# Two settling stages of a decoder step: the last tile's scale and bias moved to GpSimd, and the picking products put earlier in TensorE's order

## The chip, the cores and the metric

The program runs on one core of one Trainium2 chip. The metric is the device time of one execution in microseconds (us), and the median over runs is what counts. TensorE (PE in the profile) multiplies, VectorE (DVE), ScalarE (ACT) and GpSimd (POOL) do elementwise work, and SyncE (SP) issues most transfers.

## The reference

One inference step of a two-layer decoder trunk for 544 tokens (512 of a prompt and 8 x 4 of a sample group), 1024 wide. Each layer is a mixer, a post-norm, a hierarchical mixture of experts and a post-norm. The part that the change touches is the post-norm behind the mixer and the routing:

```python
def _layer_norm(x, g, b):
    mu = jnp.mean(xf, axis=-1, keepdims=True)
    var = jnp.mean(jnp.square(xf - mu), axis=-1, keepdims=True)
    return (xf - mu) * lax.rsqrt(var + LN_EPS) * g + b

def _hier_moe(x, w_coarse, b_coarse, w_fine, b_fine, w_gate_up, w_down):
    lc = xt @ w_coarse + b_coarse                    # 4 groups
    grp = jnp.argmax(lc, axis=-1)
    lf = einsum('nd,gde->nge', xt, w_fine) + b_fine  # 8 experts in each
    top_v, top_i = lax.top_k(lf_sel, TOP_FINE)       # 2 experts a token
    ...
    # for each expert: silu(x @ gate) * (x @ up) * gate_value, then @ w_down
```

All arrays are float32. A layer has 32 experts with 2 MB of gate and up weights and 1 MB of down weights each.

## The kernel before

`settle_and_experts` runs once in each layer (l = 0 and l = 1). Its first half, `settle_parts`, is called the settling stage here; its second half, `expert_parts`, runs the experts.

**The settling stage** goes over five tiles of tokens in the order `ORDER`: first the 32 sample rows (i = 0, tile t = 4), then four tiles of 128 prompt rows (i = 1 to 4). For each tile, PE multiplies the mixer's output by the output projection (`project`), DVE adds it to the residual (`add`) and takes the mean and variance, PE turns the tile (`flip`), ACT copies the turned tile out, and PE forms 36 router logits (`score`). ACT normalises the tile in place in two halves (L1776, semaphore `normed`), and DVE multiplies each half by gamma and adds beta (`affine`, L1596 and L1597, semaphore `final`). DVE ranks the logits into a choice of two experts (`choose`, a chain of some fifteen small instructions from L1602 to L1619, most of which read two operands in SBUF), PE counts how many tokens of the tiles so far go to each expert (`count`, L1444 and L1447), and DVE turns the counts into places (`position`) and into a one-hot matrix for the first pair of experts (`heat`, written to `G`, semaphore `hot`).

**Picking.** The first pair of experts does not wait for a gather through memory. Its 128 rows are picked out of the tiles in SBUF by one-hot products: `pick(i)` multiplies `G` of tile i with the two 512-wide halves of tile i and accumulates over the five tiles in the PSUM banks `pp[1]` and `pp[2]`. Those banks are shared with the projections: for `old` (layer 1) `pp[2]` holds the projection (3, 1) and `pp[1]` the projection (4, 1); in layer 0 it is the other way about. After `pick(4)`, ACT copies the two banks to SBUF (L1780), PE turns them (`first.x_T`, L2072), and `first.gate_up` (L2080) starts the first pair.

**The order of the engines' work is written by hand**, one list for each engine. Around the change PE's list reads: project (4, 1), flip (4, 1), a wait for `added` 8, count (3), score (4, 1), pick 0, pick 1, count (4), totals, pick 2, pick 3, pick 4, the products that wait for `tiled` (L1514, L1516), the turn, the first gate and up. DVE's list reads: choose (4), position (3), heat (3), the first half of affine (4), position (4), heat (4), the second half of affine (4), start_of (4), the tile counts (L1708, L1709), the tables. GpSimd has nothing between a memset at the start of the stage (L1386) and the first gather.

**Transfers.** SP issues the expert weights. Seven experts have room. `E.fill` loads experts 0 to 4; gate and up of experts 5 and 6 are issued when the last projection is done (`summed` 10); then SP waits for `final` of the last tile, stores its rows (L1379) and issues down of expert 5, waits for all stored rows and for `picked`, and issues down of expert 6 (L1275). From there on, `reload_up` and `reload_down` issue the weights of the next experts as PE has used the ones in their place (L1270), beginning when the first half of the first gate and up is done.

Of the kernel before, what the change touches and what calls it, by code (L numbers as in the profile page):

```python
# [15 lines left out]
ALU = mybir.AluOpType  # L16
# [8 lines left out]
ORDER = TILES[4:] + TILES[:4]  # L25
# [126 lines left out]
def tok0(t):  # L152
    return 128 * t
# [23 lines left out]
def sum_in_quarters(nc, out, N, lhsT, rhs):  # L177


    w = N // 4  # L180
    for k in range(KD):
        for q in range(4):
            last = nc.tensor.matmul(out[32 * q:32 * q + 32, 0:w], lhsT(k), rhs(k)[:, q * w:(q + 1) * w],
                                    start=(k == 0), stop=(k == KD - 1), tile_position=(0, 32 * q))
    return last
# [1121 lines left out]
def settle_parts(nc, s, place, C, X, lng, lnb, ln_T, mixT, w_dram, l, w_router, b_router, lg, xT, rows, E, back, done, ahead, first, old=None):  # L1307


    gb = E.wd[5][:, 0:2 * D].rearrange("p (a n) -> p a n", a=2)  # L1310
# [10 lines left out]
    sel, sel4, pick = place("sel", [128, 8]), place("sel4", [128, 8, 4]), place("pick", [128, 8])  # L1321
# [11 lines left out]
    G = E.xg[1][:, 0:640].rearrange("p (t n) -> p t n", t=5)  # L1333
# [6 lines left out]
    pp = ahead  # L1340

    def half_bank(i, h):
        if i == 0:
            return pp[2][:, 128 * h:128 * h + 128] if old else pp[h][:, 0:128]
        return pp[(2 * i + h - 2 if old else 2 * i + h) % 3][:, :]
# [9 lines left out]
    w_in = [s.sem(f"w_in{h}") for h in range(2)]  # L1355
    x_in = [s.sem(f"x_in{i}") for i in range(5)]
    hot, tables, picked, rows_out = (s.sem(x) for x in ("hot", "tables", "picked", "rows_out"))
    xt, x0, sl, hr = first.turned, first.x0, first.sl, first.hr

    def sync(sp):  # L1360
# [23 lines left out]

    def gpsimd(pool):
        nc.gpsimd.memset(E.xg[1][:, :], 0.0).then_inc(blank, 1)  # L1386
        pool.wait_ge(told, 1)
        pool.wait_ge(stored, 16 * 5)
        pool.wait_ge(xt, 1)
        E.rows(pool, rows, 1, s.kept[f"e{l}_rows1"])  # L1390
        pool.wait_ge(tables, 1)

    def tensor(pe):
        def project(i, h, ks):
            t, P = ORDER[i]
            if 2 * i + h < done:
                return
            if ks[0] == 0:
                pe.wait_ge(w_in[h], 16)
                if 2 * i + h >= (4 if old else 5):  # L1400
                    pe.wait_ge(added, 2 * i + h - 2)
            if t == 4:
                last = sum_in_quarters(nc, half_bank(0, h), 512, lambda k: mixT[:, k, 512:544], lambda k: w[h][:, k, :])
            else:
                for k in ks:
                    last = nc.tensor.matmul(half_bank(i, h)[:P, :], mixT[:, k, tok0(t):tok0(t) + P],  # L1406
                                            w[h][:, k, :], start=(k == 0), stop=(k == KD - 1))
            if ks[-1] == KD - 1:
                last.then_inc(summed, 1)
# [6 lines left out]
        def flip(i, h):  # L1416
            t, P = ORDER[i]
            pe.wait_ge(added, 2 * i + h + 1)
            if i >= 1:
                pe.wait_ge(T_out, 2 * i + h - 1)  # L1420
            for c in range(4):
                last = nc.tensor.transpose(pt[h][:, c * P:(c + 1) * P], X[:P, t, (4 * h + c) * 128:(4 * h + c + 1) * 128],
                                           C("ident")[:P, :P])
            last.then_inc(T_in, 1)

        def score(i, h):
            t, P = ORDER[i]
            pe.wait_ge(T_out, 2 * i + h + 1)
            if i == 0:
                pe.wait_ge(prepared_c, 1)  # L1430
            if i >= 2:
                pe.wait_ge(logit_c, i - 1)
            for k in range(4 * h, 4 * h + 4):
                last = nc.tensor.matmul(pm[i % 2][:P, 0:36], xT[:, k, tok0(t):tok0(t) + P],  # L1434
                                        wrg[:, k, :], start=(k == 0), stop=(k == KD - 1))
            if h == 1:
                last.then_inc(logits, 1)

        def count(i):
            pe.wait_ge(assigned, i + 1)  # L1440
            if i >= 1:
                pe.wait_ge(positioned, i)
            mine = A12[:, i, :]
            last = nc.tensor.matmul(pr[:, 32 * i:32 * i + 32], C("before"), mine,  # L1444
                                    start=(i == 0), stop=(i == 4), skip_group_check=True)
            for j in range(i + 1, 5):
                last = nc.tensor.matmul(pr[:, 32 * j:32 * j + 32], C("ones"), mine, start=False, stop=False,  # L1447
                                        skip_group_check=True)
            last.then_inc(ranked, 1)

        def totals():
            pe.wait_ge(logit_c, 4)
            pe.wait_ge(assigned, 5)
            for i in range(5):
                last = nc.tensor.matmul(pm[1][0:32, 0:8], A12[:, i, :], C("ones")[:, 0:8], start=(i == 0), stop=(i == 4))
            last.then_inc(counted, 1)

        def pick(i):
            t, P = ORDER[i]
            pe.wait_ge(hot, i + 1)  # L1460
            for h in range(2):
                pe.wait_ge(final, 2 * i + h + 1)
                last = nc.tensor.matmul(pp[1 + h][:, :], G[:P, i, :], X[:P, t, 512 * h:512 * h + 512], start=(i == 0), stop=(i == 4))  # L1463
                if i == 4:
                    last.then_inc(picked, 1)

# [19 lines left out]
        for i in range(2, 5):  # L1486
# [9 lines left out]
            if i < 4:  # L1496
# [2 lines left out]
        project(4, 1, second[:2])  # L1499
        score(4, 0)  # L1500
        project(4, 1, second[2:])
        flip(4, 1)
        pe.wait_ge(added, 8)
        count(3)
        score(4, 1)
        pick(0)
        pick(1)
        count(4)
        totals()
        pick(2)  # L1510
        pick(3)
        pick(4)
        pe.wait_ge(tiled, 1)
        nc.tensor.matmul(pm[0][:, 0:32], tilesT[:, 0:1].to_broadcast([32, 128]), C("before")[0:32, 0:32],  # L1514
                         start=True, stop=True)
        nc.tensor.matmul(pm[0][:, 32:64], tilesT[:, 0:1].to_broadcast([32, 128]), C("tri_p")[0:32, 0:32],  # L1516
                         start=True, stop=True).then_inc(placed, 1)
# [3 lines left out]
        for n in range(10):  # L1521
            if n in (0, 8):
                pe.wait_ge(onehots, n // 8 + 1)
            last = nc.tensor.matmul(pm[1][:, 0:NPAIR], onehot[n], ci[2][:, n, :], start=(n == 0), stop=(n == 9))
# [3 lines left out]
        for n in range(10):  # L1528
            last = nc.tensor.matmul(pr[:, 0:NPAIR], onehot[n], ci[1][:, n, :], start=(n == 0), stop=(n == 9))
# [3 lines left out]
    def vector(dve):  # L1533
# [52 lines left out]
            c.step(V.scalar_tensor_tensor(out=shift[:P, :], in0=csum[:P, :], scalar=nmr[:P, t:t + 1], in1=cbias[:P, :],  # L1586
                                          op0=ALU.mult, op1=ALU.add))

        def affine(i, halves=(0, 1)):
            t, P = ORDER[i]  # L1590
            if i == 0:
                dve.wait_ge(gb_in, 32)
            for h in halves:
                x = X[:P, t, 512 * h:512 * h + 512]
                dve.wait_ge(normed, 2 * i + h + 1)
                c.step(V.tensor_tensor(x, x, gb[:P, 0, 512 * h:512 * h + 512], ALU.mult))  # L1596
                V.tensor_tensor(x, x, gb[:P, 1, 512 * h:512 * h + 512], ALU.add).then_inc(final, 1)  # L1597
# [39 lines left out]
        def position(i):  # L1637
            t, P = ORDER[i]
            dve.wait_ge(ranked, i + 1)
            if i >= 1:  # L1640
                dve.wait_ge(positioned, i)
            c.step(V.tensor_tensor(own2[:, :, :], As[:, :, t, :],
                                   pr[:, 32 * i:32 * i + 32].unsqueeze(1).to_broadcast([128, 2, 32]), ALU.mult))
            c.add(V.tensor_reduce(rsel[:, :, t], own2[:, :, :], AX.X, ALU.add))
            V.scalar_tensor_tensor(out=slots[:, i, :], in0=pr[:, 32 * i:32 * i + 2], scalar=1.0, in1=A12[:, i, 0:2],
                                   op0=ALU.add, op1=ALU.mult).then_inc(positioned, 1)

        def heat(i):
            dve.wait_ge(positioned, i + 1)
            if i == 0:  # L1650
                dve.wait_ge(blank, 1)
            V.tensor_tensor(G[:, i, :].rearrange("p (e n) -> p e n", e=2), slots[:, i, :].unsqueeze(2).to_broadcast([128, 2, 64]),
                            C("first").unsqueeze(1).to_broadcast([128, 2, 64]), ALU.is_equal).then_inc(hot, 1)
# [44 lines left out]
        choose(4)  # L1698
        position(3)
        heat(3)  # L1700
        affine(4, (0,))
        position(4)
        heat(4)
        affine(4, (1,))
        c.wait()
        start_of(4)
        dve.wait_ge(counted, 1)
# [57 lines left out]
    def scalar(act):  # L1765
# [22 lines left out]
        act.wait_ge(tables, 1)  # L1788

    return (sync, gpsimd, tensor, vector, scalar), pt, pm, pr  # L1790


# [301 lines left out]
def settle_and_experts(nc, l, C, X, lng, lnb, ln_T, mixT, w_dram, w_router, b_router, lg, xT, xd, yd, E, back, done, ahead, old, y, y_in,  # L2094
# [3 lines left out]
    with Scope(nc, f"n{l}0") as s, Scope(nc, f"e{l}") as se:  # L2098
# [3 lines left out]
        def place(name, shape):  # L2102
# [6 lines left out]
            if len(shape) == 4:  # L2109
                return v.rearrange("p (a b c) -> p a b c", a=shape[1], b=shape[2])  # L2110
            return v

        first = FirstPair(nc, se, C, E, xT, ahead[0:2], ahead[2])
        (sync1, pool1, pe1, dve1, act1), px, py, unread = settle_parts(nc, s, place, C, X, lng, lnb, ln_T, mixT, w_dram, l, w_router,
                                                               b_router, lg, xT, xd, E, back, done, ahead, first, old)
        sync2, pool2, pe2, dve2, act2 = expert_parts(nc, se, C, X, E, xT, xd, yd, first, px, py, unread,
# [1101 lines left out]
```

## Time and profile before

| what | value |
|---|---|
| three timed runs, us | 1198.03, 1202.74, 1202.96 |
| median of the runs, us | 1202.74 |
| the profiled execution, its own time, us | 1193.56 |
| its span, first to last instruction, us | 1191.7 |
| mean granted clock of TensorE | 0.969 |
| settling stage of layer 0, its tail | about 305 to 334 us |
| settling stage of layer 1, its tail | about 891 to 920 us |

The profile is of one execution. A busy share is a mean over stages that have different limits. In the timeline a row is a run of equal instructions merged: its start, the time from the first start to the last end, engine, line, operation, tiles, shape and, in brackets, the idle time before the first of them and what ended it. PE's products and its weight loads (PEld) are separate rows. A float32 product of 512 columns is two instructions in the trace. A clock of 1.00 is 2.4 GHz, one of 0.50 is 1.2 GHz.

### The profile page before, as it was taken

What the parts mean: (1) busy time and instruction counts of PE and PEld (TensorE: products, weight loads), DVE (VectorE), ACT (ScalarE), POOL (GpSimd) and SP (SyncE); (2) the same over time, 40 slices, a digit from 0 to 9 for tenths busy, and PEclk for the clock granted to TensorE, in tenths of its full rate; (3) what the DMA queues carried; (4) which work ended last, traced back from release to release, by engine and by line L of the source; (5) the groups of instructions that cost most, each with busy time, mean ns of one, the idle gap of its engine ahead of it and who ended that gap; (6) DMA issues with size and microseconds to landing.
All of it is one profiled execution on the core that took longest, in us unless ns stands there. A gap on an engine that the chain in (4) does not pass through costs nothing. (4 is left out here: it accounts for less than half of the span.)

```text
span 1191.7 us, 15251 instructions
## 1 busy us (share of the span) xinstructions
PE 1084.7 (91%) x5783; PEld 537.6 (45%) x5783; DVE 499.2 (42%) x1368; ACT 230.8 (19%) x515; POOL 181.2 (15%) x177
## 2 busy tenths in 40 slices
PE   8999999999999998778899999999999999877972
PEld 6874555555543333222544346554545433322320
DVE  3714576668652221112562314564677322111126
ACT  0311133321121110000421122333212111000103
POOL 0000000000011120110546532230000121111113
PEclk9999999999999998899899999999999999989995
DMA  8421020439489999997989979795886999999976
GB/s 296 164 92 44 37 111 1 151 118 422 192 323 413 420 420 421 419 421 297 356 335 360 369 293 401 288 379 195 319 367 235 358 411 418 420 421 420 422 291 227
DMA packets 85068, 358.84 MB, mean 301 GB/s; under 512 B 13928, under 2 KB 18157, under 8 KB 55293
## 3 DMA queue, kind: packets, MB, share of 16 engines
q1 hardware_dynamic: 63388, 279.57, 58.9%
q0 software_dynamic: 19520, 74.01, 16.0%
q10 hardware_dynamic: 2080, 4.19, 1.0%
q8 instruction: 51, 0.84, 0.3%
q14 instruction: 29, 0.23, 0.1%
HBM read 342.75 MB, written 31.16 MB: 314 GB/s over the span
## 5 line engine op out<-in xcount | busy, mean ns | idle before, releaser
L1915 PE MATMUL ahead_psum<-m_wg,top_xT 128*64 128x512 f32 x704 | 197.8, 624 | 30.0 <-DMA m_wg<-in_moe_w_gate_up 20.9
L1915 PEld LDWEIGHTS ahead_psum<-m_wg,top_xT 128*64 128x64 f32 x704 | 60.3, 143 | 140.2 <-issue 101.1
L1940 PE MATMUL n_psum_m<-m_wd,top_xT 128*64 128x512 f32 x456 | 120.4, 598 | 1.7 <-DMA m_wd<-in_moe_w_down 0.7
L1915 PE MATMUL ahead_psum<-top_wide,top_xT 128*64 128x512 f32 x288 | 100.3, 630 | 15.1 <-DMA top_wide<-in_moe_w_gate_up 8.1
L1406 PE MATMUL ahead_psum<-top_wide,top_xT 128*128 128x512 f32 x224 | 102.1, 599 | 1.5 <-PEq L159 1.5
L1980 DVE COPY top_xT<-n_psum_t 128x512 f32<-128x512 f32 x31 | 21.4, 691 | 172.2 <-PE n_psum_t L1900 172.2
L1835 POOL DMA_INDIRECT expert_rows<-e_Y,m_dest x33 | 32.8, 995 | 366.9 <-DVE e_Y L1989 329.4
L2382 PE MATMUL ahead_psum<-top_wide,top_xT 128*128 128x512 f32 x192 | 85.4, 596 | 0.3 <-ACT top_xT L2673 0.3
L2171 POOL DMA_INDIRECT cd_kv<-in_cache_kT,top_kpages x64 | 63.7, 995 | 49.3 <-PE cd_psum_d L2425 30.4
L1940 PEld LDWEIGHTS n_psum_m<-m_wd,top_xT 128*64 128x64 f32 x456 | 34.9, 136 | 55.6 <-issue 51.8
L2031 DVE TENSOR_TENSOR top_xT<-top_xT,ahead_psum 128x256 f32<-128x256 f32 x31 | 13.0, 420 | 111.4 <-ACT top_xT L2003 108.3
L1406 PEld LDWEIGHTS ahead_psum<-top_wide,top_xT 128*128 128x128 f32 x224 | 40.5, 190 | 42.6 <-issue 42.5
L557 PE MATMUL ab_psum<-top_wide,top_xT 128*128 128x512 f32 x128 | 57.9, 601 | 0.0
L1915 PEld LDWEIGHTS ahead_psum<-top_wide,top_xT 128*64 128x64 f32 x288 | 30.0, 145 | 59.1 <-issue 40.3
L2382 PEld LDWEIGHTS ahead_psum<-top_wide,top_xT 128*128 128x128 f32 x192 | 35.4, 190 | 45.0 <-issue 44.2
L2003 ACT ACTIVATE top_xT<-ahead_psum 128x256 f32<-128x256 f32 x31 | 11.9, 384 | 189.4 <-PE ahead_psum L1915 186.2
L1386 POOL MEMSET m_xg<- 128x1024 f32 x2 | 1.9, 952 | 288.7 <-POOLq L159 288.7
L1998 ACT ACTIVATE top_xT<-ahead_psum 128x256 f32<-128x256 f32 x33 | 12.7, 384 | 169.9 <-PE ahead_psum L1926 169.9
L1302 POOL DMA_INDIRECT m_xg<-token_rows,m_tokof x15 | 15.5, 1033 | 180.5 <-DVE m_tokof L1741 176.5
L2180 POOL DMA_INDIRECT cd_kv<-in_cache_v,top_pages x32 | 30.7, 958 | 76.5 <-PE cd_psum_e L2466 52.2
L1989 DVE SCALAR_TENSOR_TENSOR e_Y<-n_psum_m,m_share,m_xg 128x512 f32<-128x512 f32 x34 | 25.5, 751 | 38.4 <-PE n_psum_m L1940 38.4
L1989 DVE SCALAR_TENSOR_TENSOR e_Y<-n_psum_m,m_share,top_X 128x512 f32<-128x512 f32 x32 | 24.0, 751 | 35.9 <-PE n_psum_m L1940 35.9
(535 smaller groups left out, 1664.9 us busy)
## 6 DMA issues: line engine op xcount, KB each, us to landing
m_wg<-in_moe_w_gate_up SPq DMA_DIRECT2D x96, 1024.0 KB, 25.3
m_wd<-in_moe_w_down SPq DMA_DIRECT2D x56, 1024.0 KB, 26.9
top_wide<-in_moe_w_gate_up SPq DMA_DIRECT2D x32, 1024.0 KB, 28.7
cd_kv<-in_cache_kT SPq DMA_DIRECT2D x64, 256.0 KB
top_X<-in_moe_w_down SPq DMA_DIRECT2D x8, 1024.0 KB, 29.0
ab_w<-in_ab_w_in SPq DMA_DIRECT2D x2, 2048.0 KB
top_wide<-in_ab_w_in SPq DMA_DIRECT2D x2, 2048.0 KB, 7.9
top_wide<-in_ab_w_out SPq DMA_DIRECT2D x2, 2048.0 KB, 9.0
```

The lines of the kernel that those rows point to most:

```text
L557: last = mm(out[:, :], xT[:, k, tok0(t):tok0(t) + 128], w[i][:, k, :], start=(k == 0), stop=(k == KD - 1))
L1302: pool.indirect_dma_start(out=self.xg[i % 4][:, :], out_offset=None, in_=xd, in_offset=bass.IndirectOffsetOnAxis(ap=self.tokof[:, i:i + 1] ...
L1406: last = nc.tensor.matmul(half_bank(i, h)[:P, :], mixT[:, k, tok0(t):tok0(t) + P], w[h][:, k, :], start=(k == 0), stop=(k == KD - 1))
L1835: nc.gpsimd.indirect_dma_start(out=yd, in_=Y[i % 2][:, :], in_offset=None, out_offset=bass.IndirectOffsetOnAxis(ap=E.dest[:, i:i + 1], axi ...
L1915: last = nc.tensor.matmul(pg[i % 2][64 * a:64 * a + 64, :], xgT[i % 2][:, j, 64 * a:64 * a + 64], wg[E.slot(i, a)][:, j * 512:(j + 1) * 51 ...
L1940: last = nc.tensor.matmul(py[n2][64 * a:64 * a + 64, :], hT[:, j, 64 * a:64 * a + 64], wd[E.slot(i, a)][:, j * D + n2 * 512:j * D + (n2 + ...
L1980: ins = nc.scalar.activation(dst, src, ACT.Copy) if half == 0 else nc.vector.tensor_copy(dst, src)
L1989: last = nc.vector.scalar_tensor_tensor(out=Y[i % 2][:, part], in0=py[half][:, :], scalar=E.share[:, i:i + 1], in1=xg[i % 4][:, part], op0 ...
L2031: nc.vector.tensor_tensor(hh, sg, pg[i % 2][:, DE:2 * DE], ALU.mult).then_inc(hr, 1)
L2171: pool.indirect_dma_start(out=self.slots[slot][:, b, 512 * j:512 * j + 512], out_offset=None, in_=self.k_rows, in_offset=bass.IndirectOffs ...
L2180: pool.indirect_dma_start(out=self.slots[slot][:, b, :], out_offset=None, in_=self.v_rows, in_offset=bass.IndirectOffsetOnAxis(ap=self.pag ...
L2382: last = nc.tensor.matmul(out[:, :], xT[:, k, tok0(t):tok0(t) + 128], w[r][:, k, :], start=(k == 0), stop=(k == KD - 1))
```

## The change

It has four parts, and all of them are made in both settling stages.

1. `affine(4)` leaves DVE. GpSimd does it: for each half it waits for `normed`, multiplies by gamma, waits for its own instruction through a new semaphore, and adds beta. These are four instructions of 128 x 512 elements.
2. One half of `pick(0)`, into the bank that is already free (the product over the half that goes to `pp[2]` in layer 1 and `pp[1]` in layer 0), stands ahead of `flip(4, 1)`, and so does the wait for `added` 8.
3. `pick(2)` stands ahead of `count(4)`. Behind `totals` only `pick(3)` and `pick(4)` are left.
4. `pick` reads all 128 partitions of `G` and of the tile, for the 32-row tile too.

```diff
+    last_scaled = s.sem("last_scaled")
...
     def gpsimd(pool):
         nc.gpsimd.memset(E.xg[1][:, :], 0.0).then_inc(blank, 1)
+        pool.wait_ge(gb_in, 32)
+        for h in range(2):
+            x, (g, b) = X[:, ORDER[4][0], 512 * h:512 * h + 512], (gb[:, a, 512 * h:512 * h + 512] for a in range(2))
+            pool.wait_ge(normed, 9 + h)
+            nc.gpsimd.tensor_tensor(x, x, g, ALU.mult).then_inc(last_scaled, 1)
+            pool.wait_ge(last_scaled, h + 1)
+            nc.gpsimd.tensor_tensor(x, x, b, ALU.add).then_inc(final, 1)
         pool.wait_ge(told, 1)
...
-        def pick(i):
+        def pick(i, halves=(0, 1)):
             t, P = ORDER[i]
             pe.wait_ge(hot, i + 1)
-            for h in range(2):
+            for h in halves:
                 pe.wait_ge(final, 2 * i + h + 1)
-                last = nc.tensor.matmul(pp[1 + h][:, :], G[:P, i, :], X[:P, t, 512 * h:512 * h + 512], start=(i == 0), stop=(i == 4))
+                last = nc.tensor.matmul(pp[1 + h][:, :], G[:, i, :], X[:, t, 512 * h:512 * h + 512], start=(i == 0), stop=(i == 4))
...
         project(4, 1, second[2:])
+        pe.wait_ge(added, 8)
+        pick(0, (1,) if old else (0,))
         flip(4, 1)
-        pe.wait_ge(added, 8)
         count(3)
         score(4, 1)
-        pick(0)
+        pick(0, (0,) if old else (1,))
         pick(1)
+        pick(2)
         count(4)
         totals()
-        pick(2)
         pick(3)
         pick(4)
...
         heat(3)
-        affine(4, (0,))
         position(4)
         heat(4)
-        affine(4, (1,))
         c.wait()
         start_of(4)
```

## Rows read from the trace of the kernel before

**Rows 1.** The page, part 1: busy time, share of the span, instructions.

```profile
PE 1084.7 (91%) x5783; PEld 537.6 (45%) x5783; DVE 499.2 (42%) x1368; ACT 230.8 (19%) x515; POOL 181.2 (15%) x177
```

**Rows 2.** The chain that ended last, in order of time, layer 1's tail: start, duration, what.

```profile
907.90 0.27 DVE top_lg L1602
...
912.33 0.38 PE n_psum_r L1444 x2
912.71 0.41 PE n_psum_m L1455 x10
913.12 5.36 PE ahead_psum L1463 x12
918.50 0.61 ACT m_xg L1780
```

**Rows 3.** The timeline of layer 1's tail, all engines.

```profile
905.36 0.66 PE L1422 MATMUL n_psum_t<-top_consts,top_X 128*128 128x128 f32 x4 [0.78 <-DVE top_X L1551]
...
907.22 1.52 ACT L1776 ACTIVATE top_X<-top_X,e_Y 128x512 f32<-128x512 f32 x2 [0.48 <-DVE e_Y L1575]
...
907.72 3.89 PE L1463 MATMUL ahead_psum<-top_X,m_xg 32*128 32x512 f32 x8
...
908.19 0.17 DVE L1226 TENSOR_TENSOR e_Y<-top_lg 128x16 f32<-128x16 f32 x1
...
909.31 0.20 DVE L1608 TENSOR_TENSOR e_Y<-top_lg,e_Y 128x32 f32<-128x32 f32 x1
...
912.33 0.38 PE L1444 MATMUL n_psum_r<-e_Y,top_consts 128*128 128x32 f32 x2 [0.71 <-DVE e_Y L1645]
912.42 0.68 DVE L1596 TENSOR_TENSOR top_X<-top_X,m_wd 128x512 f32<-128x512 f32 x1
...
915.25 0.69 DVE L1597 TENSOR_TENSOR top_X<-top_X,m_wd 128x512 f32<-128x512 f32 x1
...
915.97 0.33 SPq L1379 DMA_DIRECT2D token_rows<-top_X  x1
...
924.78 6.74 SPq L1270 DMA_DIRECT2D m_wg<-in_moe_w_gate_up  x4
```

**Rows 4.** The timeline of layer 0's tail, PE alone.

```profile
321.85 5.54 PE L1463 MATMUL ahead_psum<-top_X,m_xg 32*128 32x512 f32 x8
...
327.23 0.31 PE L1444 MATMUL n_psum_r<-e_Y,top_consts 128*128 128x32 f32 x2
```

**Rows 5.** Windows of 1 us: busy time by engine, PE's clock, DMA share, GB/s.

```profile
322.00:323.00 1.00, 1.00 (x3) 0.51 (x4) 0.86 (x5) 0.88 (x2) 0.00 (x0) 1.00 1.01 426
...
324.00:325.00 1.00, 1.00 (x3) 0.48 (x3) 0.90 (x5) 0.00 (x0) 0.00 (x0) 0.50 0.99 418
```

**Rows 6.** GpSimd's groups of instructions by line and shape.

```profile
L204 POOL TENSOR_TENSOR m_wg<-m_wg 128x1024 f32<-128x1024 f32 x4 | 9.4, 2344 | 9.3 <-DMA m_wg<-expert_rows 9.2
L2331 POOL TENSOR_TENSOR cd_kv<-cd_kv 128x1024 f32<-128x1024 f32 x3 | 7.1, 2355 | 13.4 <-DMA cd_kv<-expert_rows 13.3
```

**Rows 7.** The timeline of the last stage, VectorE and GpSimd.

```profile
1179.24 2.35 POOL L204 TENSOR_TENSOR m_wg<-m_wg 128x1024 f32<-128x1024 f32 x1 [0.16 <-DMA m_wg<-expert_rows]
...
1180.09 1.28 DVE L279 SCALAR_TENSOR_TENSOR top_X<-m_wg,n_mv,n_psum_g 128x1024 f32<-128x1024 f32 x1
...
1183.05 1.28 DVE L279 SCALAR_TENSOR_TENSOR top_X<-m_wg,n_mv,n_psum_g 128x1024 f32<-128x1024 f32 x1
```

**Rows 8.** The timeline of PE among the experts: sixteen equal products after idle time.

```profile
434.19 3.65 PE L1915 MATMUL ahead_psum<-m_wg,top_xT 128*64 128x512 f32 x16 [1.86 <-DMA m_wg<-in_moe_w_gate_up]
...
483.70 5.35 PE L1915 MATMUL ahead_psum<-m_wg,top_xT 128*64 128x512 f32 x16 [4.47 <-DMA m_wg<-in_moe_w_gate_up]
...
1065.77 6.24 PE L1915 MATMUL ahead_psum<-m_wg,top_xT 128*64 128x512 f32 x16 [4.78 <-DMA m_wg<-in_moe_w_gate_up]
```

**Rows 9.** Windows of 10 us among the experts, columns as in rows 5.

```profile
370.00:380.00 10.00, 10.00 (x52) 3.97 (x50) 1.86 (x3) 1.37 (x3) 2.02 (x2) 1.00 1.01 417
...
960.00:970.00 10.00, 10.00 (x52) 3.99 (x50) 2.19 (x3) 0.98 (x2) 1.58 (x2) 1.00 1.01 416
```

More of the change, by code:

```diff
@@ L1587, in shift_of, with affine @@
                                           op0=ALU.mult, op1=ALU.add))
-        def affine(i, halves=(0, 1)):
+        def affine(i):
             t, P = ORDER[i]
@@ L1592, in affine @@
                 dve.wait_ge(gb_in, 32)
-            for h in halves:
+            for h in range(2):
                 x = X[:P, t, 512 * h:512 * h + 512]
```

## The prediction

> **What bounds the kernel now.** I read the page's first part, then the chain that ended last, then the timeline at the place of the change. PE is busy 91% of the span and GpSimd 15% [rows 1], but a mean says nothing about one stage. The chain in order of time does: in the settling stage's tail it passes through VectorE's choice (it enters it at 907.90), through PE's last count, the totals and the twelve instructions of pick 2 to 4, and into ACT's copy at 918.50 [rows 2]. Behind that come the turn and the first gate and up, whose first half releases the first reload of weights at 924.78 [rows 3]. Some 35 us later the DMA engines are full, at 416 to 417 GB/s, and stay so nearly to the end of the experts, in both layers [rows 9]; PE then waits for weights. So the tail counts because it sets when the reloads begin: a microsecond there moves the whole stream of weights by about one, and this happens twice, once in each layer. What PE loses or gains once the stream is full costs nothing.
>
> **Half of pick 0 ahead of the last turn.** Its matrix and its half were ready long before, and its bank is free. PE stands idle for 0.78 us ahead of the turn, waiting for VectorE's add [rows 3]. A picking product is two instructions, and twelve instructions take 5.36 us [rows 2], of which some 0.2 is the last one's tail, so one is 0.43 and the half is 0.86. It covers the gap and reaches 0.08 past it. The turn, the logits and the choice start 0.08 later. Cost: +0.08 a stage.
>
> **Pick 2 ahead of the last count.** Pick 0 and 1 run from 907.72 for 3.89 us, to 911.61; then PE is idle for 0.71 until VectorE's position (L1645) releases the count at 912.33 [rows 3]. After the change five products, ten instructions, stand there: 4.3 us from 907.80, to 912.1. That fits ahead of 912.33. Behind the totals eight instructions are left in place of twelve: −4 x 0.43 = −1.73 us a stage. This is the gain, and it holds only while the count is released no later than before.
>
> **All rows read.** Eight instructions took 3.89 rather than 8 x 0.43 = 3.44 [rows 3]; the 0.45 is a pause where 32 partitions turn into 128. It goes, but into a stretch where PE waits for VectorE anyway: nothing, apart from making pick 2 fit.
>
> **Affine 4 leaves VectorE.** There it was four instructions of 0.68 and 0.69 [rows 3], 2.8 us, half of them under PE's last count, the rest under its picks. VectorE's later work (position 4, heat 4, the tile counts) comes earlier by 0.8 to 2.1 us; PE reaches the products that read it only after pick 4, so this gives nothing by itself, but it keeps up with the shorter picks. SP's store of the last tile, now at 915.97 [rows 3], follows GpSimd.
>
> **Affine 4 on GpSimd.** A tensor_tensor of 1024 columns takes 2.34 to 2.36 us there [rows 6]; of 512 I take half, 1.17. ACT's two normalised halves begin at 907.22 and take 1.52 together [rows 3], so the first is out at 907.98. Four instructions with 0.1 to 0.15 between them are done at about 913.2. Pick 4 would want its last half at about 915.8, so GpSimd itself is in time by 2.5 us. The first gather queued behind it waits for later things.
>
> **What it does to VectorE** is the disputed price. The four instructions run from 908.07 to 913.2, on top of the choice, which is on the path and whose instructions mostly read two operands in SBUF (L1226 at 908.19 to L1608 and on) [rows 3]. The trace has GpSimd arithmetic only beside VectorE instructions with at most one such operand: L279, whose second operand is in PSUM, takes 1.28 beside a running L204 and 1.28 without one [rows 7]. So this trace shows no price for two operands. The lower bound is nothing, by rows 7. The upper one is that neither engine runs while the other does, so that VectorE waits out each GpSimd instruction. L1226, due at 908.27, then waits to 909.25; it and L1227 slip through between multiply and add; L1228 waits for the add, L1229 for the second multiply, and L1608 for the second add, to 913.4 in place of 909.31. That is +4.1 us for the choice; with no slipping through it is 5. I take the upper bound, 4.1: two streams of operands for each engine are nearest to a case of full exclusion, and the row that shows no price has only one stream. The rule that I weigh against rows 7 is in the Trainium skill, "SBUF — State Buffer", Who interferes with whom: a VectorE instruction with two SBUF inputs and a GpSimd instruction that reads SBUF exclude each other for the whole instruction. By it the sum is the upper bound's; by the plain reading of rows 7 it is the lower's. No row here tests it.
>
> Then the count starts at 912.33 + 4.1 = 916.4, and the net of the stage is +4.1 − 1.73 = **+2.4 us** (the 0.08 is lost in rounding).
>
> **The clock.** PE would be idle from 912.1 to 916.4, 4.3 us. Among the experts the sixteen products that take 3.65 us after an idle time of 1.86 take 5.35 after 4.47 and 6.24 after 4.78 [rows 8]: the granted clock fell to 1.2 GHz. So idle time of this length costs 1.7 to 2.6 more, here on the path; I take 1.7. In layer 0 a fall is there already: the clock was 1.00 at 322 and 0.50 at 324 [rows 5], the four products took 5.54 [rows 4] in place of 3.89, and the count began 5.38 behind the first pick in place of 4.61 [rows 3, 4], 0.77 late, which I take off.
>
> **Sum.** 2 x (2.4 + 1.7) − 0.7 = **+7.5 us** against the profiled execution: 1193.6 + 7.5 = 1201.1. That execution is 9 us below the median of the three runs, 1202.7. The same 7.5 on the median gives **1210** us, 0.6% slower.
>
> **Rivals.**
>
> A, the forecast: the engines exclude each other and the clock falls. +5.5 to +11 (the upper end with a wait of 5 and a fall of 2.6: 2 x (5 − 1.7 + 2.6) − 0.7). For it: the choice overlaps all four GpSimd instructions, and has more than enough two-operand steps to meet each. Against it: no row shows the exclusion. Chance 0.42.
>
> B, they hinder each other in part, or the clock stays up: a wait of 1.7 to 4.1 without a fall, 0 to +5 us. The point that decides the sign is a delay of the choice by 1.65 us a stage, one and a half GpSimd instructions. Chance 0.14.
>
> C, the other side: they run freely beside each other. Then each stage gains 1.73 − 0.08 = 1.65, 3.3 in all, and up to 4.0 if pick 0 in PE's gap also keeps layer 0's clock up: 1198.7 to 1199.4 on the median. For it: rows 7. Its gain is under 0.5%. Chance 0.38.
>
> D, the gain does not reach the end or GpSimd is late (over 1.8 us for one instruction makes pick 4 wait): −1 to +1. Against it: rows 6 and the full stream [rows 9]. Chance 0.06.
>
> **How the numbers follow.** The three runs lie within 5 us, 0.4%; about 0.5%, 6 us, is what a measurement of this kernel can tell from no change. Slower by more than that is nearly all of A: 0.42. Faster by more than that needs C and something that I have not priced, or a lucky set of runs: 0.12. The rest is 0.46. The range reaches from C with 1.5 us for the runs' spread, 1197, to A with the wider wait and fall, 1214. By itself A gives 1208 to 1214, C 1197 to 1201.
>
> **What the profile after would show.** For the forecast: L1226, L1228 or their like starting only as a GpSimd row on the new lines ends; the choice (L1602 to L1619) taking about 8 us in place of 3.8; PE idle for some 4 us ahead of the last count; a clock of 0.50 in the picks behind it. For C: the choice as long as before, the count within 0.1 us of its old place, ACT's L1780 1.65 earlier. The GpSimd rows should be 1.1 to 1.3 us each; at 2 us or more both sums are wrong. The flip of the last half should start less than 0.2 us after VectorE's add ends. The time from ACT's last copy to the first reload should be what it was, 6.3 us [rows 2, 3]; otherwise the tail is not where the difference was made. The prediction is wrong above all if the exclusion is not there, or if a wait ends in the middle of a GpSimd instruction.

## The result and the profile after

The changed kernel takes 1209.84 us, median of 6 runs (1208.4 to 1210.7); the kernel before, 1202.85, median of 6. The ratio is 1.0052, 95% interval 1.0027 to 1.0077: **slower by 6 to 7 us**, 0.5 to 0.6% (3.2 to 9.3 us by the interval). The prediction was 1210, and 7.5 us for the difference. The ratios leave out executions in a slower state of the chip, of which affine_back_2 had one, at 2127 us.

The timeline of the changed kernel in layer 1's tail, which answers to [rows 3]. Line numbers have moved: L1596 and L1597 of `affine` are L1605 and L1606, GpSimd's new lines are L1392 (multiply) and L1394 (add), pick is L1471, the last count L1452.

```profile
912.81 0.66 PE L1430 MATMUL n_psum_t<-top_consts,top_X 128*128 128x128 f32 x4
...
914.67 1.52 ACT L1783 ACTIVATE top_X<-top_X,e_Y 128x512 f32<-128x512 f32 x2 [0.48 <-DVE e_Y L1584]
...
915.06 4.54 PE L1471 MATMUL ahead_psum<-top_X,m_xg 128*128 128x512 f32 x10
...
915.63 0.17 DVE L1226 TENSOR_TENSOR e_Y<-top_lg 128x16 f32<-128x16 f32 x1
915.63 1.30 POOL L1392 TENSOR_TENSOR top_X<-top_X,m_wd 128x512 f32<-128x512 f32 x1 [70.18 <-ACT top_X L1783]
915.72 1.24 DVE L1227 TENSOR_TENSOR e_Y<-top_lg 128x16 f32<-128x16 f32 x1
917.00 0.17 DVE L1228 TENSOR_TENSOR e_Y<-e_Y,top_consts 128x16 f32<-128x16 f32 x1
917.01 1.29 POOL L1394 TENSOR_TENSOR top_X<-top_X,m_wd 128x512 f32<-128x512 f32 x1
917.21 1.13 DVE L1229 TENSOR_TENSOR e_Y<-e_Y 128x16 f32<-128x16 f32 x1
918.26 1.26 POOL L1392 TENSOR_TENSOR top_X<-top_X,m_wd 128x512 f32<-128x512 f32 x1
918.37 0.17 DVE L1230 TENSOR_REDUCE e_Y<-e_Y 128x4 f32<-128x16 f32 x1
918.57 0.98 DVE L1616 TENSOR_SCALAR e_Y<-e_Y 128x4 f32<-128x4 f32 x1
919.59 0.20 DVE L1617 TENSOR_TENSOR e_Y<-top_lg,e_Y 128x32 f32<-128x32 f32 x1
919.60 1.30 POOL L1394 TENSOR_TENSOR top_X<-top_X,m_wd 128x512 f32<-128x512 f32 x1
...
920.05 0.93 DVE L1226 TENSOR_TENSOR e_Y<-e_Y 128x64 f32<-128x64 f32 x1
...
923.33 0.38 PE L1452 MATMUL n_psum_r<-e_Y,top_consts 128*128 128x32 f32 x2 [3.72 <-DVE e_Y L1654]
...
924.18 5.19 PE L1471 MATMUL ahead_psum<-top_X,m_xg 128*128 128x512 f32 x8
...
935.67 6.74 SPq L1270 DMA_DIRECT2D m_wg<-in_moe_w_gate_up  x4
```

The reader is to see that L1227, L1229 and L1616, of 16 or 4 elements a partition, which took 0.17 us, now take 1.24, 1.13 and 0.98, that the second L1226, of 64 elements, takes 0.93 in place of 0.22, and that each of the four ends with a GpSimd instruction, within 0.1 us. A blocked instruction counts as busy, so a list of idle times would not have shown it: VectorE has no idle row here. Idle time appears one engine further on, 3.72 us of PE ahead of the last count. Behind it eight instructions take 5.19 us, where ten took 4.54 a moment before.

Layer 0's tail is the same, with the full length of the forecast: L1226, L1228, L1229 and L1616 take 1.29, 1.22, 1.19 and 1.09 us there.

```profile
330.38 0.60 PE L1452 MATMUL n_psum_r<-e_Y,top_consts 128*128 128x32 f32 x2 [4.29 <-DVE e_Y L1654]
...
331.55 6.24 PE L1471 MATMUL ahead_psum<-top_X,m_xg 128*128 128x512 f32 x8
```

Windows of 1 us there (columns as in rows 5), in PE's idle time and after it: the granted clock goes from 1.00 to 0.50.

```profile
328.00:329.00 1.00, 0.00 (x0) 0.00 (x0) 0.86 (x6) 0.00 (x0) 0.00 (x0) 1.00 0.95 401
...
332.00:333.00 1.00, 1.00 (x2) 0.39 (x2) 0.86 (x7) 0.00 (x0) 0.00 (x0) 0.50 1.02 430
```

GpSimd's groups after, which answer to [rows 6]:

```profile
L1394 POOL TENSOR_TENSOR top_X<-top_X,m_wd 128x512 f32<-128x512 f32 x4 | 5.1, 1277 | 0.3
L1392 POOL TENSOR_TENSOR top_X<-top_X,m_wd 128x512 f32<-128x512 f32 x4 | 5.1, 1273 | 135.1 <-ACT top_X L1783 135.1
```

**A measure for one tail.** From the issue of the last gate and up load of the fill, which SP makes as the last projection ends, to the first reload (the first and the last SP row of the tail): 20.86 and 20.16 us before (layer 0, layer 1), 25.55 and 23.62 after. So the two tails give 4.7 + 3.5 = 8.2 us. From the start of ACT's last copy to the first reload it is 6.27 or 6.28 us in both kernels and both layers, so the difference lies ahead of that copy. The profiled spans differ by more, 1206.2 − 1191.7 = 14.5; the rest lies elsewhere. The execution profiled before was 9 us under its own median, the one after less than 2.

### The profile page after: what moved, and what is told of

Read it like the earlier page. It is cut to its first block and busy times, and to the rows that moved or that the text cites. A ratio compares the mean times of both kernels' runs of the same rounds, so it can differ in the third digit from the quotient of the medians.

```text
span 1206.2 us, 15255 instructions
## 1 busy us (share of the span) xinstructions
PE 1094.3 (91%) x5783; PEld 542.1 (45%) x5783; DVE 502.0 (42%) x1360; ACT 230.7 (19%) x515; POOL 191.2 (16%) x185
## 5 line engine op out<-in xcount | busy, mean ns | idle before, releaser
L1947 PE MATMUL n_psum_m<-m_wd,top_xT 128*64 128x512 f32 x456 | 123.8, 614 | 1.6 <-ACT top_xT L2005 1.0
L2010 ACT ACTIVATE top_xT<-ahead_psum 128x256 f32<-128x256 f32 x31 | 11.9, 383 | 187.2 <-PE ahead_psum L1922 187.2
L557 PEld LDWEIGHTS ab_psum<-top_wide,top_xT 128*128 128x128 f32 x128 | 23.4, 190 | 28.8 <-issue 27.0
```

The source lines that it names most:

```text
L557: last = mm(out[:, :], xT[:, k, tok0(t):tok0(t) + 128], w[i][:, k, :], start=(k == 0), stop=(k == KD - 1))
L1947: last = nc.tensor.matmul(py[n2][64 * a:64 * a + 64, :], hT[:, j, 64 * a:64 * a + 64], wd[E.slot(i, a)][:, j * D + n2 * 512:j * D + (n2 + ...
```

## The experiments

The table has, for each kernel, the length of the choice of the last tile, PE's idle time ahead of the last count, the tail as measured above (layer 0 / layer 1 each time), and the ratio to the kernel before with its interval. Each length is from one profiled execution. Three kernels ran once and have no ratio.

| kernel | choice, us | PE idle, us | tail, us | ratio |
|---|---|---|---|---|
| before | 3.83 / 3.83 | 0 / 0.71 | 20.86 / 20.16 | 1 |
| after | 7.94 / 7.38 | 4.29 / 3.72 | 25.55 / 23.62 | 1.0052 (1.0027 to 1.0077) |
| affine_back | 3.84 / 3.84 | 0.19 / 0.18 | 18.84 / 18.83 | 0.9965 (0.9941 to 0.9988) |
| affine_back_2 | 3.84 / 3.83 | 0.19 / 0.18 | 18.84 / 18.83 | 0.9948 (0.9919 to 0.9977) |
| gpsimd_alone | 7.94 / 7.38 | 2.19 / 2.62 | 27.07 / 25.33 | 1.0086 (1.0055 to 1.0117) |
| kept_clock | 7.94 / 7.39 | 0.86 / 0.29 | 22.58 / 22.00 | 1.0016 (0.9993 to 1.0039) |
| one_half | 6.01 / 5.88 | 2.36 / 2.21 | 22.30 / 20.49 | 1.0013 (0.9991 to 1.0035) |
| write_only | 4.06 / 4.07 | 0.41 / 0.41 | 19.06 / 19.07 | one execution |
| read_one | 5.90 / 5.90 | 2.25 / 2.24 | 22.22 / 21.21 | one execution |
| after_choice | 3.84 / 3.84 | 0.19 / 0.18 | 19.98 / 22.87 | 0.9970 (0.9951 to 0.9989) |
| rows_alone | 3.85 / 3.83 | 1.06 / 0 | 20.19 / 20.57 | one execution |
| half_ahead_alone | 3.84 / 3.84 | 0.44 / 0 | 22.19 / 23.44 | 0.9984 (0.9960 to 1.0008) |
| pick2_alone | 3.84 / 3.84 | 0 / 0 | 22.55 / 22.55 | 0.9992 (0.9965 to 1.0019) |
| slots_first | 3.84 / 3.84 | 0 / 0 | 18.61 / 20.30 | 0.9965 (0.9946 to 0.9984) |

**affine_back**: the change without its first part.

```diff
 # the changed kernel; GpSimd's four instructions and their waits go as well
         heat(3)
+        affine(4, (0,))
         position(4)
         heat(4)
+        affine(4, (1,))
```

> The changed kernel with the last tile's scale and bias back on VectorE, where it was before; the other three parts stay (half of pick 0 ahead of the turn, pick 2 ahead of the last count, all rows read). Exclusion theory: no GpSimd row in the tail, so the choice takes about 3.7 us again in both layers, PE waits under 0.4 us for the last count, the clock stays at 1.00, and ACT's first copy of the picked rows starts 1.7 us earlier than before relative to the turn; 3.3 to 4 us faster than before in time, so about 10 us faster than the change. Rival, that the cost comes from the new order of the picks on PE (the half pick ahead of the turn, or three picks in a row ahead of the count): then this stays slower than before, by up to 7 us. Second rival, that a shorter tail doesn't reach the end: same as before within 1 us.

The choice is back at 3.84 us and the tails are 2.0 and 1.3 us below before's. PE alone, layer 1:

```profile
901.50 4.54 PE L1463 MATMUL ahead_psum<-top_X,m_xg 128*128 128x512 f32 x10
906.22 0.38 PE L1444 MATMUL n_psum_r<-e_Y,top_consts 128*128 128x32 f32 x2 [0.18 <-DVE e_Y L1646]
...
906.94 4.07 PE L1463 MATMUL ahead_psum<-top_X,m_xg 128*128 128x512 f32 x8
```

This kernel is faster than both. Both rivals fall: the three parts on PE help, and the time is shorter by 4.2 us (1.3 to 7.0). Repeated on another chip it was faster again:

> The kernel of affine_back again, to be compared on one chip with the next three. Expected from the first time: the tails (last projection's end to the first reload of weights) 18.8 us each, 2.0 and 1.3 below before; the time 3 to 5 us below before.

**gpsimd_alone**: the kernel before with GpSimd's `affine(4)` and nothing else.

```diff
 # the kernel before
+        pool.wait_ge(gb_in, 32)
+        for h in range(2):
...
+            nc.gpsimd.tensor_tensor(x, x, g, ALU.mult).then_inc(last_scaled, 1)
...
+            nc.gpsimd.tensor_tensor(x, x, b, ALU.add).then_inc(final, 1)
-        affine(4)
```

> The kernel before with one part of the change alone: the last tile's scale and bias on GpSimd. Exclusion theory: the choice is 3.5 to 4.1 us longer, PE is idle for 4.3 to 4.8 us ahead of the last count (pick 2 isn't there to fill 0.8 of it), the clock falls, and all six picking products stand behind the count at 1.2 GHz: about 1.7 us a stage worse than the change, so 10 to 11 us slower than before. Rival (the order of the picks costs the time): same as before, or up to 1 us faster because VectorE has less to do.

The choice lengths are those of the changed kernel to 0.01 us, and the kernel is 0.86% slower, 10 us, as expected. The first part alone makes the whole loss. PE's idle time was 2.2 to 2.6 us rather than the 4.3 to 4.8 expected, because the clock had already fallen during pick 0 and 1, which took 6.54 and 5.54 us.

**one_half** (in the changed kernel, GpSimd does the first half only, two instructions in place of four):

```diff
-        for h in range(2):
+        for h in (0,):
...
         heat(4)
+        dve.wait_ge(final, 9)
+        affine(4, (1,))
```

> The changed kernel with the first half of the last tile's scale and bias on GpSimd (two instructions in place of four), and the second half on VectorE behind its last position. Exclusion theory: the delay of the choice goes with the number of GpSimd instructions, so it is about 2.0 us in place of 4.1 and 3.6, PE is idle for about 2 us, which is too short for the clock to fall; each stage comes out 0.3 us worse than before: the same as before within 1.5 us. Rival (a fixed cost of starting GpSimd arithmetic in the tail, such as code loading): the delay stays near 4 us and the time 6 to 7 us above before.

The choice is 2.2 and 2.05 us longer than before's: half of 4.1 and of 3.6, within 0.3. The delay goes with the number of GpSimd's instructions; a fixed cost could be 0.2 to 0.6 us of it, not 4. In one point the expectation failed: after 2.36 us idle the clock did fall in layer 0, and the eight instructions took 5.37; after 2.21 in layer 1 it did not, and they took 3.70.

**write_only** and **read_one** put other GpSimd work of similar length into the same stretch of affine_back.

```diff
 # write_only
+        for h in range(2):
+            pool.wait_ge(normed, 9 + h)
+            for n in range(6):
+                nc.gpsimd.memset(E.xg[1][:, 640:1024], 0.0).then_inc(filled[h], 1)
+                pool.wait_ge(filled[h], n + 1)
 # read_one, in place of the memset
+                nc.gpsimd.tensor_copy(E.xg[1][:, 640:1024].rearrange("p (a n) -> p a n", a=3),
+                                      C("ident").unsqueeze(1).to_broadcast([128, 3, 128])).then_inc(filled[h], 1)
```

> The kernel of affine_back with twelve GpSimd memsets of 128 x 384 (results unused) in the stretch where the change has its four tensor_tensor: GpSimd is as busy, but reads nothing from SBUF. Theory that VectorE's second operand needs the read path that GpSimd reads through: the two-operand instructions of the choice keep their 0.17 to 0.22 us, and only instructions of one SBUF operand that may use both paths (L1616, L1621) can be longer; the choice stays at 3.7 to 4.3 us. Rival, that any GpSimd instruction shuts VectorE's two-operand instructions out: they end only with a memset, and the choice takes over 5 us.

> As write_only, but with twelve GpSimd tensor_copy of 128 x 384, which read one operand from SBUF. Theory of the shared read path, held for a whole instruction: VectorE's two-operand instructions of the choice wait for the copy in progress (each of the copies costs up to its own length, some 0.4 us), and the choice takes 6 to 8 us. Rival, that only two-operand instructions on both sides exclude each other: the choice stays at 3.7 us.

The timelines of layer 0's choice, write_only first (its memsets run from 322.10 to 327.75), then read_one:

```profile
322.21 0.17 DVE L1226 TENSOR_TENSOR e_Y<-top_lg 128x16 f32<-128x16 f32 x1
...
323.12 0.37 DVE L1614 TENSOR_SCALAR e_Y<-e_Y 128x4 f32<-128x4 f32 x1
```

```profile
321.94 0.43 DVE L1226 TENSOR_TENSOR e_Y<-top_lg 128x16 f32<-128x16 f32 x1
...
323.39 0.17 DVE L1614 TENSOR_SCALAR e_Y<-e_Y 128x4 f32<-128x4 f32 x1
323.59 0.54 DVE L1615 TENSOR_TENSOR e_Y<-top_lg,e_Y 128x32 f32<-128x32 f32 x1
```

GpSimd works all through the choice in both, with twelve memsets of 0.42 us or twelve copies of 0.51. Beside memsets, which read nothing, every two-operand instruction keeps its length and the choice costs 0.2 us more, all of it in a one-operand instruction. Beside copies the two-operand ones that meet a copy stretch to as much as 0.54, the others keep 0.16 or 0.17 (L1227 and L1229 in layer 0), and the choice takes 5.9, a little less than the 6 to 8 expected. So it is GpSimd's reading that shuts VectorE's second operand out. The Trainium skill, "SBUF — State Buffer", Who interferes with whom, states this, with the exemption for writing; by that rule these two traces agree.

**kept_clock** fills PE's idle time in the changed kernel.

```diff
         pick(2)
+        for _ in range(4):
+            nc.tensor.matmul(pt[0][:, :], C("ident"), X[:, ORDER[1][0], 0:512], start=True, stop=True)
         count(4)
```

> The changed kernel with four more products (unused results, 3.4 us at full clock) on PE between pick 2 and the last count, where it stands idle for 4.3 and 3.7 us. It does the same work otherwise. Theory that the idle time lets the clock fall and that this costs on its own: the clock stays at 1.00 behind the count, the eight instructions of pick 3 and 4 take 3.6 us in place of 6.2 and 5.2, and the time is 3 to 4 us less than the change's (3 to 4 us slower than before). Rival (the clock's fall is hidden by something else that waits, the weights' stream for one): the picks get shorter but the time stays at the change's, 7 us slower than before.

The picks behind the count, layer 0, against 6.24 in the changed kernel:

```profile
330.70 3.70 PE L1471 MATMUL ahead_psum<-top_X,m_xg 128*128 128x512 f32 x8
```

The tails lose 3.0 and 1.6 us, 4.6 in all, and the ratio goes from 1.0052 to 1.0016, which is 4.3 us. The clock is a cost of its own. That it reaches the end rests on the tails and the time together: the intervals of the two ratios overlap (1.0027 to 1.0077, 0.9993 to 1.0039).

**after_choice** holds GpSimd, in the changed kernel, until the choice is done.

```diff
         pool.wait_ge(gb_in, 32)
+        pool.wait_ge(assigned, 5)
         for h in range(2):
```

> The changed kernel with GpSimd's four instructions held until the choice of the last tile is done. Exclusion theory: the choice takes 3.7 us again and the count comes on time; GpSimd's 5.2 us then end 5.3 us behind the choice, where pick 4 wants its last half about 4 us behind it, so PE waits some 1.3 us there, and VectorE's two-operand instructions behind the choice (heat, start_of) are hit, position 4 and heat 4 some 1 to 2 us late: each stage comes out between 0.5 us better than before and 1 us worse, the time within 2 us of before. Rival, that GpSimd's arithmetic costs the same wherever it stands in the tail: 7 us slower, as the change.

The same four instructions in another place: the choice takes 3.84, the count comes on time, and the kernel is faster than before by 0.3%. PE waits for the last add, 0.96 us in layer 1:

```profile
920.43 1.13 PE L1472 MATMUL ahead_psum<-top_X,m_xg 128*128 128x512 f32 x2 [0.96 <-POOL top_X L1395]
```

So the place decides, not the work. Layer 0's tail is 1.1 us longer than affine_back's; the times (0.9970 and 0.9965) do not tell the two apart. In layer 1 the clock fell behind the picks, after gaps that were the same as layer 0's to 0.01 us: the sixteen instructions of the first gate and up took 6.05 us in place of 3.65, hence 22.87. The two tails together are then 1.8 us longer than the profiled ones of before, though the time is shorter; what this says of that profile stands under the clock below.

**The other parts one by one**, each put into the kernel before.

```diff
 # rows_alone
-                last = nc.tensor.matmul(pp[1 + h][:, :], G[:P, i, :], X[:P, t, 512 * h:512 * h + 512], ...
+                last = nc.tensor.matmul(pp[1 + h][:, :], G[:, i, :], X[:, t, 512 * h:512 * h + 512], ...
 # half_ahead_alone
+        pe.wait_ge(added, 8)
+        pick(0, (1,) if old else (0,))
         flip(4, 1)
-        pe.wait_ge(added, 8)
...
-        pick(0)
+        pick(0, (0,) if old else (1,))
 # pick2_alone
+        pick(2)
         count(4)
-        pick(2)
```

> The kernel before with one part of the change alone: the picks read all 128 partitions for the 32-row tile too. Expected: the pause of 0.45 us between pick 0 and pick 1 goes, the eight instructions take 3.5 us in place of 3.9, PE waits 1.1 us in place of 0.7 for the last count, and nothing behind it moves. Rival, that a product over 128 partitions takes longer than one over 32: eight instructions still take 3.9 us or more.

> The kernel before with one part alone: half of pick 0 ahead of the turn. Expected: PE's idle time ahead of the turn goes and the turn starts no later; the picks ahead of the count end 0.9 us earlier, to no use. Theory on the clock: that idle time is what lets the clock fall in this place in some executions (in 4 of 6 tails without the half ahead, in none of 14 with it), so here it stays at 1.00 in both layers, both tails take 20.1 to 20.2 us, and the time is 0 to 1.5 us below before. Rival: the falls are chance, and one of the two tails shows one.

> The kernel before with one part alone: pick 2 ahead of the last count, with pick 0 whole behind the logits and read in 32 rows. Theory: the six products take 5.6 us from 3.1 us behind the last projection's end, so the count starts at 8.7 in place of 7.7, and 1.7 us fewer are left behind it: the tail is 0.7 us shorter than before's, 19.4 where the clock holds, and the clock can fall as before (then 21 or more). Time within 2 us of before. Rival: the parts add up, each giving its share of the 1.7 us whatever the others do; then this one gives all of it, a tail of 18.5 us.

Reading all rows shortens the eight instructions of pick 0 and 1 in layer 0 to 3.68 us from 3.89, not to the 3.5 expected, and starts them 0.09 earlier; in layer 1 the clock fell in them. The half alone, in 32 rows, delays the turn by 0.2 us, and the expectation about the clock failed outright: it fell in both layers. Pick 2 alone stands in a stretch at half clock in both layers, and the count comes 11.9 us behind the last projection in place of 7.7. Layer 0 of the two, PE alone:

```profile
322.31 4.19 PE L1463 MATMUL ahead_psum<-top_X,m_xg 32*128 32x512 f32 x6
```

```profile
321.51 8.96 PE L1463 MATMUL ahead_psum<-top_X,m_xg 32*128 32x512 f32 x12
```

The rival that each part gives its share is wrong in the traces: by it pick2_alone's tails would be 18.5 us, and they are 22.55. Over all profiled tails, the clock fell during the picks ahead of the count in 8 of 10 where the half was not ahead of the turn or the picks read 32 rows, and in none of the 18 that had both. Neither part alone held it in both layers. The count was made afterwards, and why the two together hold the clock stays open. In time half_ahead_alone and pick2_alone are the same as before, though their tails are 4 to 5 us longer in sum; the falls may differ from one execution to the next, and one profile does not show how often.

**slots_first** changes VectorE's order in affine_back: the slots of tiles 3 and 4, `scalar_tensor_tensor` of `position`, come ahead of the rest of it.

```diff
-        position(3)
+        place_slots(3)
         heat(3)
         affine(4, (0,))
-        position(4)
+        place_slots(4)
         heat(4)
         affine(4, (1,))
+        position(3, False)
+        c.wait()
+        position(4, False)
```

> The kernel of affine_back with VectorE's list changed in the tail: of position 3 and position 4 only the instruction that the one-hot matrix and the count need stands where it was, the two others of each are moved behind the last tile's second half. Theory that VectorE's order sets both remaining waits of PE: the count starts 0.2 us earlier, right behind pick 2, and pick 4 no longer waits 0.4 us for its last half; the tail is 0.4 to 0.6 us shorter than affine_back's, 18.3, and the time about 1 us less, which the rounds can't tell from nothing. Rival: the moved instructions now delay the tile counts, PE waits for them behind the picks, and the tail stays at 18.8.

The count starts 0.36 us earlier and pick 4 no longer waits, but layer 0's tail is only 0.2 shorter, since PE now waits for the moved instructions (0.66 us ahead of L1515, released by L1721). So the theory holds for the two waits that were to go, and the rival for the one that comes in their place. In layer 1 the clock fell in the first gate and up (5.35 us in place of 3.65), which costs more than that. On the same chip affine_back_2 has 0.9948 and this 0.9965, within each other's interval. The change shows no gain.

## Why the prediction was right, point by point

**VectorE shut out.** Forecast from the upper bound: +4.1 us on the choice, four GpSimd instructions each met by one of VectorE's. Measured: 7.94 − 3.83 = 4.11 in layer 0 and 3.55 in layer 1. The choice between the two bounds was right, and affine_back, gpsimd_alone, one_half and after_choice show it from four sides. Two details were off. In layer 0 the order is the forecast's step by step (L1226 waits, L1227 slips through, L1228 and L1229 wait), but the fourth wait fell on L1616 in place of L1617; L1616 has one SBUF operand, a kind that the forecast left out. In layer 1 L1226, L1228 and L1617 started within 0.01 us of a GpSimd instruction and passed, so that the four that waited met theirs 0.09 to 0.45 us after its start, in place of 0.01 to 0.20, and the delay is 0.56 shorter.

**GpSimd in time.** 1.27 to 1.28 us each in place of 1.17, done at 920.90 in layer 1; pick 4's last half started 7.4 us later, where the forecast had 2.5, because the picks themselves came later.

**Pick 2 ahead of the count.** −1.73 us forecast. affine_back, which has this without the loss, starts ACT's copy 1.70 us earlier than before in layer 1 (11.32 behind the last projection, 13.02 before). The tail as a whole gained 1.3 only, because pick 4 then waits 0.4 for its last half.

**Half of pick 0.** +0.08 forecast, 0.02 measured: the turn starts 0.76 behind the projection's end (912.81 − 912.05) against 0.74.

**All rows read.** This is where the prediction was wrong in kind. It priced this part at nothing. half_ahead_alone shows that without it the half ahead costs 0.2 us, and the count of falls shows that the two together go with a held clock. The pause of 0.45 us was mis-sized too: 8 x 0.43 leaves out the last instruction's tail of 0.2, and rows_alone has the picks end 0.3 us earlier, 0.1 of it in their start.

**The clock behind the idle time.** 1.7 us a stage forecast; 6.24 − 3.70 = 2.5 in layer 0, 5.19 − 3.70 = 1.5 in layer 1, 4.6 with what follows by kept_clock, against 3.4. The term taken off for layer 0, 0.7, was 0.77 in the trace, but it describes one execution. affine_back gains 4.2 and 6.3 us in time with tails that are only 3.4 us shorter than the profiled ones of before, which fits if most executions of the kernel before lose more to the clock than the profiled one.

Two things on record point that way. The mean granted clock was 0.969 in the profiled execution of before and 0.960 to 0.962 in the median of its later timed ones, against 0.965 and 0.966 for affine_back. And a straight line through the ten rows of the table with a ratio, before's own left out (sum of the two tails, time by the ratio), rises by 1.0 us for 1 us of tail and reaches a ratio of 1 at 43.8 us, 2.8 above the 41.0 of before's profile; single rows lie up to 3.7 us off it. The 43.8 is an estimate from one profile for each kernel; the tails of a typical execution of before were not measured.

**The sum.** +7.5 forecast, 8.2 in the tails, 7.0 in time (3.2 to 9.3 by the interval). The near agreement of the last is partly luck: 0.7 more in the tails, and a reference execution that was not typical. The prediction carried the 7.5 from that execution over to the median. Against tails of 43.8 us, 3.5 above two without a fall (2 x 20.16), its own terms would have given 2 x 4.1 − 3.5 = 4.7.

## What to carry to other kernels

Before work goes to GpSimd from a busy VectorE, look at what VectorE does in that stretch. Beside a chain of tiny two-operand instructions each GpSimd instruction that reads cost most of its length here (4.1 and 3.6 us for 5.1 us of GpSimd), and one kind with a single SBUF operand (L1616) was held up too; the reductions in the same chain, also of one operand, kept their 0.17 to 0.19. A blocked instruction looks busy: search for instructions that are longer than their shape, not for gaps. When a stall of some microseconds on TensorE is priced, price the clock behind it too. And a difference worked out from one profiled execution holds against that execution: see first how far it lies from the median.

## What the runs showed of the hardware

- A 128x4 tensor_scalar with one SBUF input took 1.09 and 0.98 us beside a GpSimd tensor_tensor, and 0.37 beside memsets of 0.42, where it takes 0.17 alone. Of the choice's instructions it is the only one that a memset held up. Beside the copies it took 0.17.
- Whether TensorE's clock falls is not decided by the length of one gap. In after_choice the gaps of the two layers agree to 0.01 us (the longest is 0.97), and it fell in layer 1 alone; in slots_first too, where the longest is 0.78. In the kernel before and its variants it fell in some tails during a dense run of picks behind gaps of 0.78 and 0.32 us. After 2.36 and 2.25 us of idle time it fell, and after 2.21 and 2.24 it did not.
- Where products over 32 partitions follow or precede ones over 128, PE loses some tenths: the eight instructions of pick 0 and 1 end 0.3 us earlier when all read 128 (3.68 us from 3.01 behind the last projection in rows_alone's layer 0, against 3.89 from 3.10 in layer 1 of the kernel before), and the turn behind a half of 32 partitions starts 0.2 later than behind one of 128.
